# Encoder trunk on one core: expert rows fetched by indirect DMA instead of selection products, attention heads in pairs, logits with tokens on the partitions

## What is computed

```
logits = t @ w_router + b_router            # 256 tokens, 8 experts
top_val, top_idx = top_k(logits, 2); gates = softmax(top_val)
each expert e, on the tokens that chose it:
    y = (silu(x @ w_gate[e]) * (x @ w_up[e])) @ w_down[e]     # 3584 columns
out[token] += gate * y
```

## Time and profile before

| | |
|---|---|
| median of 3 runs | 1401.43 us (1401.04 to 1401.51) |
| the profiled execution, its own time | 1400.22 us |
| its span | 1398.0 us |
| busy: TensorE, VectorE, ScalarE, POOL | 1375.8, 1130.9, 926.2, 20.0 us |
| DRAM read | 419.12 MB |
| expert part, first gather to the end of the span | 405.0 to 1398.0 us |

### The profile page before, as it was taken

One profiled execution on the slowest core, in us unless ns is written; L12 is line 12 of the kernel. 1 busy time (PEld: TensorE's weight loads), 2 busy tenths in 40 slices (PEclk: granted clock), 3 DMA queues, 4 the chain that ended last, 5 costly groups with the idle time before them and its releaser, 6 DMA issues.

```text
span 1398.0 us, 17684 instructions
## 1 busy us (share of the span) xinstructions
PE 1375.8 (98%) x6463; PEld 1140.4 (82%) x6463; DVE 1130.9 (81%) x823; ACT 926.2 (66%) x760; POOL 20.0 (1%) x29
## 2 busy tenths in 40 slices
PE   9999999999979999999999999999999999999997
PEld 8888888787858888888888888888888888888885
DVE  5756666655578889888988988898898889889887
ACT  6454433545557777777777777777777777777774
POOL 0000000000120000000000000000000000000000
PEclk9999999999999999999999999999999999999999
DMA  9576775551339999999999999999999999999992
GB/s 351 205 207 191 220 218 185 169 189 66 96 122 346 371 377 327 372 371 353 354 369 369 333 368 376 349 355 370 373 328 367 377 346 351 376 371 334 375 377 87
DMA packets 191961, 420.76 MB, mean 301 GB/s; under 512 B 19184, under 2 KB 21616, under 8 KB 191920
## 3 DMA queue, kind: packets, MB, share of 16 engines
q1 hardware_dynamic: 178704, 415.65, 82.5%
q10 hardware_dynamic: 12784, 3.26, 1.7%
q0 software_dynamic: 432, 1.28, 0.3%
HBM read 419.12 MB, written 1.05 MB: 301 GB/s over the span
## 4 chain that ended last, share of the span: by engine, by line
PE 96%; DVE 2%; ACT 1%; DMA 1%; issue 0%; POOL 0%; SPq 0%; POOLq 0%; DVEq 0%; ACTq 0%
PE bank_G L1097 10%; PE bank_G L1099 10%; PE bank_G L1098 10%; PE bank_U L1097 10%; PE bank_U L1099 10%; PE bank_U L1098 10%; PE bank_Y L1097 8%; PE bank_Y L1099 8%; PE bank_Y L1098 8%; PE bank_T L1463 2%; PE bank_G L1355 1%; PE bank_T L1097 1%; PE bank_T L1099 1%; PE bank_T L1098 1%; PE bank_T L1366 1%; DMA raw<-in_fourier_w_in 1%
## 5 line engine op out<-in xcount | busy, mean ns | idle before, releaser
L695 DVE TENSOR_TENSOR w_lo<-raw,w_hi 128x2048 fp32r<-128x2048 f32 x390 | 888.0, 2290 | 192.9 <-ACT w_hi L414 192.8
L414 ACT ACTIVATE w_hi<-raw 128x2048 fp32r<-128x2048 f32 x390 | 748.2, 1919 | 278.9 <-PE bank_U L1099 101.9
L1097 PE MATMUL bank_Y<-w_hi,hidT_hi 128*128 128x512 f32 x492 | 192.3, 391 | 0.0
L1099 PE MATMUL bank_Y<-w_hi,hidT_lo 128*128 128x512 f32 x492 | 191.6, 389 | 0.0
L1098 PE MATMUL bank_Y<-w_lo,hidT_hi 128*128 128x512 f32 x492 | 191.5, 389 | 0.0
L1097 PE MATMUL bank_U<-w_hi,xg_hi 128*128 128x512 f32 x448 | 179.1, 400 | 0.0
L1097 PE MATMUL bank_G<-w_hi,xg_hi 128*128 128x512 f32 x448 | 175.2, 391 | 0.7 <-DVE w_lo L695 0.5
L1099 PE MATMUL bank_U<-w_hi,xg_lo 128*128 128x512 f32 x448 | 175.0, 391 | 0.0
L1098 PE MATMUL bank_U<-w_lo,xg_hi 128*128 128x512 f32 x448 | 174.6, 390 | 0.0
L1099 PE MATMUL bank_G<-w_hi,xg_lo 128*128 128x512 f32 x448 | 174.6, 390 | 0.0
L1098 PE MATMUL bank_G<-w_lo,xg_hi 128*128 128x512 f32 x448 | 174.3, 389 | 0.0
(11 more groups left out here) (274 smaller groups left out, 1445.4 us busy)
## 6 DMA issues: line engine op xcount, KB each, us to landing
raw<-in_expert_w_gate SPq DMA_DIRECT2D x112, 1024.0 KB, 7.0
raw<-in_expert_w_up SPq DMA_DIRECT2D x112, 1024.0 KB, 7.0
raw<-in_expert_w_down SPq DMA_DIRECT2D x112, 1024.0 KB, 6.8
raw<-in_nat_w_qkv SPq DMA_DIRECT2D x12, 1024.0 KB, 5.2
raw<-in_ffn_w_gate SPq DMA_DIRECT2D x11, 1024.0 KB, 8.5
raw<-in_ffn_w_up SPq DMA_DIRECT2D x11, 1024.0 KB, 6.2
raw<-in_ffn_w_down SPq DMA_DIRECT2D x11, 1024.0 KB, 5.3
raw<-in_fourier_w_in SPq DMA_DIRECT2D x4, 1024.0 KB, 11.5
```

The source lines that it names most:

```text
L414: nc.scalar.activation(w_hi[w][:], raw[s][:], ACT.Copy).then_inc(hi_made, 1)
L695: nc.vector.tensor_tensor(w_lo[w][:], raw[s][:], w_hi[w][:].bitcast(f32), ALU.subtract).then_inc(lo_made, 1)
L1097: nc.tensor.matmul(out_, xh, wh, start=start, stop=False)
L1099: return nc.tensor.matmul(out_, xl, wh, start=False, stop=stop)
```

## The change

The gain of the norm no longer goes into the operand of the first gather: the raw stream is split (`token_hi`, `token_lo`), the norm's factor of each slot comes by two small products (`rstd_of_slots`) and is applied in silu and in the product with up. VectorE writes the normalised rows to `hn` behind the first expert's third low part, and POOL writes them once to a tensor in DRAM, with a row of zeros behind. In experts 0 to 6, two products with two columns give the token number of each slot of the next expert (`token_numbers`), VectorE turns them into row indices, and POOL fetches 128 rows by an indirect DMA straight into `xg`. The products of `gather` remain for the first expert and the second sweep. Attention runs over pairs of heads: the scores of both heads alternately, then two transposes, then two value products, with four `probT` buffers instead of two. The logits are made with the tokens on the partitions, high and low weights side by side as 16 columns. Filler products (`keep_warm`) stand in the router. At the start the first piece is loaded in quarters between the halves of x, and its split alternates with that of x. The diff, cut:

```diff
+    rows = nc.dram_tensor("token_rows", [S + 1, D], f32, kind="Internal").ap()
...
+        def first_piece(part):
+
+            src, tiles, _ = dense[0]
+            done = raw_in[0] if part == PARTS - 1 else s_first[part]
+            sp.dma_start(raw[0][:, BANK * part:BANK * (part + 1)], src[:, part]).then_inc(done, 16)
+
...
         for c in range(2):
             cs = slice(BANK * c, BANK * (c + 1))
             sp.dma_start(fo["x_turns"][:, :, cs], x[0, :, cs].rearrange("(p b) d -> p b d", b=NB)).then_inc(s_x[c], 16)
+            first_piece(2 * c)
+            first_piece(2 * c + 1)
         for j, (src, tiles, _) in enumerate(dense):
-            load(j, None, src, tiles)
+            if j:
+                load(j, None, src, tiles)
...
-        pool.wait_ge(s_gain, 32)
-        for c in range(2):
-            pool.wait_ge(h_half, 4 + c + 1)
-            cs = slice(BANK * c, BANK * (c + 1))
-            nc.gpsimd.tensor_tensor(hn[:, :, cs], h[:, :, cs], mo["gain"][:, 0:1, cs].to_broadcast([P, NB, BANK]),
-                                    ALU.mult).then_inc(hn_done, 1)
         rstds(3)
-
-        nc.gpsimd.tensor_scalar(mo["gain"][:, 1], mo["gain"][:, 1], float(D) ** 0.5, None, ALU.mult).then_inc(fin_gain, 1)
+        nc.gpsimd.memset(mo["no_row"][:], 0.0).then_inc(no_row_made, 1)
+        pool.wait_ge(hn_made, NB)
+        pool.dma_start(rows[0:S, :].rearrange("(b p) d -> p b d", p=P), hn[:]).then_inc(s_rows, 16)
+        pool.wait_ge(no_row_made, 1)
+        pool.dma_start(rows[S:S + 1, :], mo["no_row"][:]).then_inc(s_rows, 16)
+        pool.wait_ge(s_rows, 32)
+        for E in range(LAST):
+            pool.wait_ge(e_row, E + 1)
+            pool.wait_ge(e_xT, 2 * E + 2)
+            nc.gpsimd.indirect_dma_start(mo["xg"][:], None, rows, bass.IndirectOffsetOnAxis(ap=mo["row"][:, 0:1], axis=0)).then_inc(s_xg, 16)
+
...
-        stream_hi(0, 0)
-        for part in range(PARTS):
-            split_part(0, part)
-        stream_hi(0, 1)
-        for part in range(PARTS):
-            split_part(1, part)
+        for n in range(2):
+            for quarter in range(2):
+                stream_hi(0, n, [quarter])
+                split_part(n, 2 * quarter)
+                split_part(n, 2 * quarter + 1)
...
+        for p in range(PAIRS + 1):
+            if p == PAIRS:
+                output_hi(0)
+                output_hi(1)
+            if p:
+                for g in (2 * p - 2, 2 * p - 1):
+                    act.wait_ge(a_pT, g + 1)
+                    if g >= PROBS:
+                        act.wait_ge(a_pv, g - PROBS + 1)
+                    nc.scalar.activation(att["probT"][:, g % PROBS], T[g % 2][:], ACT.Copy).then_inc(a_pTcopy, 1)
+            if p < PAIRS:
...
+        def token_hi(c):
+
+            cs = slice(BANK * c, BANK * (c + 1))
+            for b in range(NB):
+                nc.scalar.activation(mo["hn_hi"][:, b, cs], h[:, b, cs], ACT.Copy).then_inc(hnr_hi, 1)
...
+        act.wait_ge(h_half, 5)
+        token_hi(0)
+        for b in range(NB):
+            nc.scalar.activation(mo["y_hi"][:, BANK * b:BANK * (b + 1)], h[:, b, :BANK], ACT.Square,
+                                 accum_out=mo["sumsq_half"][:, b:b + 1]).then_inc(sq_half, 1)
+        act.wait_ge(h_half, 6)
+        token_hi(1)
         stream_hi(3, 1)
-        squares(3)
...
-        for b in range(NB):
-            nc.scalar.activation(mo["hn_hi"][:, b], hn[:, b], ACT.Copy, scale=rstd[:, 3, b:b + 1]).then_inc(hnr_hi, 1)
+
...
-            nc.scalar.activation(silu_g[c % 2][:], G[c % 2][:], ACT.Silu).then_inc(e_silu, 1)
+            nc.scalar.activation(silu_g[c % 2][:], G[c % 2][:], ACT.Silu, scale=mo["rstd_of_slot"][:, 0:1]).then_inc(e_silu, 1)
...
-        for i in range(HEADS):
-            dve.wait_ge(a_score, i + 1)
-            if i >= 2:
...
+        for p in range(PAIRS):
+            for i in (2 * p, 2 * p + 1):
+                dve.wait_ge(a_score, i + 1)
+                if i >= 2:
+                    dve.wait_ge(a_exp, NB * (i - 1))
+                nc.vector.scalar_tensor_tensor(out=silu_g[i % 2][:].rearrange("p (n k) -> p n k", n=NB), in0=two(G[i % 2]),
+                                               scalar=float(HD) ** -0.5, in1=head_bias(i), op0=ALU.mult, op1=ALU.add).then_inc(a_biased, 1)
...
+        def token_lo(c, b):
+
+            cs = slice(BANK * c, BANK * (c + 1))
+            dve.wait_ge(hnr_hi, NB * c + b + 1)
+            rest(mo["hn_lo"][:, b, cs], h[:, b, cs], mo["hn_hi"][:, b, cs]).then_inc(hnr_lo, 1)
...
         add_projection(at["wo"], ao_psum, WO[0], 0)
-        split_past(W0 + 2)
+        split_past(W0 + 3)
         stream_lo(3, 0)
+        token_lo(0, 0)
+        token_lo(0, 1)
+        dve.wait_ge(s_rout, 64)
+        nc.vector.tensor_copy(mo["token"][:].rearrange("p b n -> p (b n)"), mo["count"][:, S:S + 2 * NB]).then_inc(token_made, 1)
+        nc.vector.tensor_copy(mo["before_h"][:], mo["before"][:]).then_inc(before_done, 1)
+        nc.vector.tensor_scalar(mo["below"][:], mo["count"][:, 0:NE], -float(NE), None, ALU.add).then_inc(before_done, 1)
...
         add_projection(at["wo"], ao_psum, WO[1], 1)
+
+        dve.wait_ge(h_half, 6)
+        for b in range(NB):
+            dve.wait_ge(sq_half, b + 1)
+            half = h[:, b, BANK:]
+            nc.vector.tensor_tensor_reduce(out=mo["xg"][:, BANK * b:BANK * (b + 1)], in0=half, in1=half, scale=1.0,
+                                           scalar=mo["sumsq_half"][:, b:b + 1], op0=ALU.mult, op1=ALU.add,
+                                           accum_out=sumsq[:, 3, b:b + 1]).then_inc(sq_done, 1)
...
+        token_lo(1, 0)
+        dve.wait_ge(rstd_done, 4)
         dve.wait_ge(logit_psum, 1)
...
-            link(nc.vector.scalar_tensor_tensor(out=mo["logit"][:, b], in0=G[1][:, NE * b:NE * (b + 1)], scalar=rstd[:, 3, b:b + 1],
-                                                in1=mo["rb"][:], op0=ALU.mult, op1=ALU.add))
+            nc.vector.scalar_tensor_tensor(out=mo["rest"][:, b], in0=G[b][:, NE:2 * NE], scalar=rstd[:, 3, b:b + 1],
+                                           in1=mo["rb"][:], op0=ALU.mult, op1=ALU.add).then_inc(low_added, 1)
+        for b in range(NB):
...
+            link(nc.vector.tensor_tensor(mo["cand"][:], below, mo["eq"][:], ALU.mult))
             link(nc.vector.tensor_reduce(mo["idx"][:, n], mo["cand"][:], AX.X, ALU.min))
-            link(nc.vector.tensor_scalar(mo["idx"][:, n], mo["idx"][:, n], float(NE), None, ALU.add))
-            link(nc.vector.tensor_tensor(mo[one][:], iota, each_token(mo["idx"][:, n]), ALU.is_equal))
+            link(nc.vector.tensor_tensor(mo[one][:], below, each_token(mo["idx"][:, n]), ALU.is_equal))
...
         def gather_copy(E1):
-            dve.wait_ge(e_gather, 2 * E1)
-            nc.vector.tensor_copy(mo["xg"][:, BANK:], U[1][:]).then_inc(e_xg_dve, 1)
-
-        def gather_lo(E1):
+
             for q in range(2):
+                cs = slice(BANK * q, BANK * (q + 1))
+                dve.wait_ge(e_gather, 2 * by_products(E1) - 1 + q)
+                if isinstance(E1, int) and E1 == 1:
+                    made_copy = nc.vector.tensor_tensor(mo["xg"][:, cs], (G, U)[q][1][:], mo["gain"][:, 0, cs], ALU.mult)
+                else:
+                    made_copy = nc.vector.tensor_copy(mo["xg"][:, cs], (G, U)[q][1][:])
+                made_copy.then_inc(e_xg[q], 1)
+
+        def row_numbers(E):
+
+            dve.wait_ge(e_token, E + 1)
+            nc.vector.tensor_scalar(mo["row"][:], T[1][:, BANK - 2:BANK - 1], float(S), None, ALU.add).then_inc(e_row, 1)
+
+        def first_rstd():
+
+            dve.wait_ge(e_rstd, 1)
+            nc.vector.tensor_copy(mo["rstd_of_slot"][:], T[1][:, BANK - 1:BANK]).then_inc(e_rstd_copy, 1)
+
+        def rstd_is_one(E):
+
+            dve.wait_ge(e_hid, E * STEPS + STEPS)
+            nc.vector.tensor_copy(mo["rstd_of_slot"][:], mo["ones"][:, 0:1]).then_inc(e_rstd_copy, 1)
+
...
-        token_rest(0)
-        token_rest(1)
+        token_lo(1, 1)
+        dve.wait_ge(s_gain, 32)
+        gather_copy(1)
+        first_rstd()
+        gather_lo(1)
...
+        assert made[0] == N1
+        for j in range(SPLIT, AHEAD):
+            split_lo(j, 0)
+        for b in range(NB):
+            nc.vector.scalar_tensor_tensor(out=hn[:, b], in0=h[:, b], scalar=rstd[:, 3, b:b + 1], in1=mo["gain"][:, 0],
+                                           op0=ALU.mult, op1=ALU.mult).then_inc(hn_made, 1)
...
+                            pe.wait_ge(act_lo_done, kk // 2 + 1)
...
         pe.wait_ge(still_made, 1)
-        still(14)
+        still(10)
         pe.wait_ge(s_ident, 16)
         transpose_stream(0, 0)
-        transpose_stream(0, 1)
...
+        def pair_scores(p):
+
+            pe.wait_ge(a_biased, 2 * p)
+            for b in range(NB):
+                for half in range(2):
+                    p0, n = HD * half, NB - 1 - b
```

(94 more changed lines are left out.)

285 lines of the change are left out of this document (133 added, 152 removed).

## The result

The changed kernel takes **1384.4 us** (median of 4 runs, 1383.5 to 1385.03) against 1401.47 us (4 runs, 1401.04 to 1403.09) for the kernel before on the same chip: a ratio of 0.9879, 95% interval 0.9864 to 0.9894. The profiled execution took 1385.03 us with a span of 1383.2 us, 14.8 us less than the span before.

What follows compares the result with a forecast made beforehand. TensorE, busy for 98% of a 1398.0 us span, was taken as the bound. Savings of 11.1 + 5.1 + 0.7 - 0.1 = 16.8 us gave 1383.4 profiled and a median of 1384.6 us; range 1379 to 1393.

Steps and rivals of the forecast that it cites:

- Loop: Expert loop: seven of eight experts lose their eight gather products on TensorE, net 1.59 us each, 11.1 us saved.
- The token products: Expert loop: two added two-column products for the token numbers cost TensorE 0.11 us each, 0.22 per expert.
- Attention: Attention: alternating two heads' score products overlaps some passes, saving 6.4 us, less 1.3 of stalls: 5.1 us saved.
- they overlap fully: Attention rival: score products of two heads overlap fully, 8.5 us for 8 pairs, total 1382.5 us; chance 0.08.
- The stalls: Attention, first slots: copies ahead of pair 1's exponentials and late transposes cost 0.8 + 0.5 = 1.3 us.
- Router and first expert: Last output projection to first expert: fillers hold the clock, VectorE's added work delays TensorE; 0.1 us lost net.
- First gate to resumption: First expert: TensorE resumes 13.5 us after the first gate product instead of 11.9, as VectorE's low part comes later.
- Start: Start: first weight piece lands in quarters, so the first product starts near 9.7 us; 0.7 us saved.
- DMA rival: Expert loop: DMA engines become the bound at 359.8 GB/s, an expert takes 123.8 us, total 1405.4 us; chance 0.05.

Runs made afterwards that it cites:

- Early fillers: Changed kernel with filler products on TensorE from the first logit groups until behind the rank products, ahead of the clock's fall: 1380.66 us.
- moved vector work: Changed kernel with VectorE's normalised rows and small weight operations moved into its waits, out of the way of the first expert's w_lo: 1380.99 us.
- four fetches: Changed kernel with each of the 7 indirect fetches issued four times, one after the other has landed, into the same tile: 1383.56 us.
- products in the loop: Changed kernel with the 8 gather products put back into each of the 7 loop passes, their sums unused: 1396.73 us.

## Why the prediction was right, and where it was not

The forecast of 1384.6 us lies 0.2 us from the median, with two terms off in opposite directions, attention by 2.5 us and the router by 4.9. In the profiled span the terms sum to 14.8 us instead of 16.8; the medians of the two kernels are 17.1 us apart because the profiled execution of the changed kernel was the slowest of its four and that of the kernel before was 1.2 us under its median. That the time fell inside the range follows from the loop and attention; that it lies within 0.2 us of the forecast is luck.

- **Loop**, right: period 120.8 (120.8 forecast), transposes directly behind the down products, no new wait, 370 GB/s. The token products cost 0.14 us per expert (425.25 to 425.39), not 0.22. Putting the products back cost 12.3 us, taking them out saved 11.5.
- **Attention**, mechanism right, size wrong. The step that failed is "Passes of one product use the same rows and can't overlap; in the new order, with starts in order, only the last pass of a product and the first of the next can". The starts of a pair are not in order: the passes run as two strands, one per half of the rows, and eight take 1.07 us instead of my 1.33. The gross gain is 8 x 1.06 = 8.5, the rival "they overlap fully", to which I had given 0.08. The Trainium skill, "TensorE: Matmul & The Clock Gate", Part 3, says that such products run concurrently, and the trace agrees: two passes start within 0.1 us, and the run that kept the heads apart lost 8.5 us. The stalls, forecast 1.3 in the first slots, were 0.65 and 0.33 there and 0.28 before the last value projection. That leaves 7.2 of the measured 7.6 us; the transposes and value products of a pair also take 0.1 us less than before (2.75 instead of 2 x 1.43), which I had put at nothing.
- **Router and first expert**, wrong. The step was "The added filler products keep it working; if 2.4 GHz stays granted the gather takes 1.8 us instead of 3.4". I asked whether fillers would hold the clock, not where it would fall. It fell ahead of them, between the two halves of the short logit products that this same change had made, so the second half became slow as well. That the shortness of these products brings it down is likely, since the wide ones of before did not, but no run parts it from the waits around them. From the transposes of the attention outputs the first gate product came 1.7 us later than before (34.67 us against 32.98), not 1.5 earlier. First gate to resumption took 13.45 us (13.5 forecast, 11.88 before), but I read it as a plain delay; it is also a wait of 2.04 us, and a second slow stretch follows it here, worth 1.7 us, which no term of the sum had. The 5.0 us lost lie far outside the term's own bounds, 1.5 lost to 1.5 gained, and in the total only the surplus of 2.5 in attention and the 2.3 us between medians and profiled executions hid it. Early fillers and moved vector work gave 3.7 and 3.4 us alone, and 5.8 to 6.0 together, more than the 5.0 that the stretch had lost.
- **Start**, right in size (0.75 for 0.7), and the first product starts at 9.52 (9.7 forecast); how the gain divides is not shown.
- **DMA rival**, out: 370 GB/s in the loop and 383 with four fetches. The Trainium skill, "DMA: Bandwidth & Descriptors", section "Where 436 GB/s comes from", would have the bound at about 358 GB/s per core, which it works out as half of what two cores share. Here one core runs alone, and its loop moved more. The rival's 1405.4 us counts the gain of 5.7 elsewhere as kept (1401.4 + 9.7 - 5.7), though its sentence calls it lost.

## What to carry to other kernels

When products are made narrower, look at the clock as well as at their time. Here fillers helped only where they stood ahead of the place at which the granted clock fell and ran through to the end of the thin stretch, and a trace shows where that is. Work that is put onto an engine at a change of stage should be placed in that engine's own waits, even if nobody waits for its result, since it delays what stands behind it. Where a term rests on two products running side by side, look at starts in a narrow window of the trace, for the order in the program says little about them.

## What the runs showed of the hardware

Score products on different halves of the rows ran side by side even where another product of the first head stood between them in the program: the eight passes still took 1.07 us. The busy share does not tell the clock: TensorE shows as busy for 2.50 of 2.50 us in the second half of the logits, at a granted clock of 0.50. The clock also fell at the end of an idle stretch of 3.39 us, while in the same stretch filled with products it stayed at 1.00. Three executions with the same instructions in the router (the changed kernel, products in the loop, four fetches) had slow stretches of different length, with the first gate product at 404.58, 404.80 and 403.06 us, and the second of them had no second slow stretch: two traces of one sequence can differ by some 1.7 us through the clock alone. An indirect fetch of 128 rows of 4 KB took GpSimd 0.94 to 1.03 us to issue, and up to 1.75 us in the run with four.
